# Another order of the query tiles in two causal attentions of a decoder trunk

## The chip, the core and the metric

The kernel runs on one core of one Trainium2 chip. The core has a matrix engine (TensorE, PE in the profile; PEld is its weight load), a vector engine (VectorE, DVE), a scalar engine (ScalarE, ACT), GpSimd (POOL) and a queue engine that issues most DMAs (SyncE, SP). Each engine runs its own instructions in their written order and waits on semaphores for the others. The metric is the device time of one launch in microseconds; lower is better.

## The reference, cut to what matters

Two decoder layers (DEPTH = 2) over 1024 positions of width 1024. Each layer is an RMSNorm, one input projection, four groups of heads side by side (Mamba-2 SSD, sparse attention "dsa", latent attention "mla", forgetting attention "fox"), an output projection with a residual, and a mixture of experts. The change touches mla and fox, which have four heads each and compute

```python
def one(i):                       # one tile of 128 queries
    start = i * Q_BLOCK           # Q_BLOCK = 128
    q_blk = lax.dynamic_slice_in_dim(q, start, Q_BLOCK, axis=1)
    logits = jnp.einsum('bqhd,bkhd->bhqk', q_blk, k) * scale
    ...                           # fox adds f_q - f_k
    mask = k_pos[None, :] <= q_pos[:, None]
    p = jax.nn.softmax(jnp.where(mask, logits, -jnp.inf), axis=-1)
    return jnp.einsum('bhqk,bkhd->bqhd', p, v)
```

The tiles are independent of each other. Tile t sees (t+1)·128 keys, so tile 7 is eight times as wide as tile 0.

## The kernel before, in words

A layer runs in phases with a barrier between them (PHASE, L293): projections and SSD, dsa, the latent up-projection (mla_proj, L935 to L948), then mla and fox as one run of `attend("mla", "fox")`, a barrier (phase "fox"), the output projection (L965) and the experts.

`attend` is written three times, once for each of PE (L729), ACT (L1121) and DVE (L1481). All three walk the same list `units` of (kind, tile t, head h), 64 entries for mla and fox: kind outermost, then tile, then head. Place u of the list does this:

- PE, `logits(u)`: the product of queries and keys for (t+1)·128 columns, in pieces of up to 512 (L753), and the diagonal mask (L758). It goes to one of two banks (`PS[n % 2]`), so it first waits until ACT has read the logits of place u-2 (L747, `lg_taken`).
- DVE: the row maximum over all (t+1)·128 columns (L1512) and its scaling (L1513).
- ACT: the exponential with its sum (L1151), which frees the bank (L1155).
- PE, `turn_p(u)`: t+1 transposes of 128x128 (L683), in turns of up to four. The turns go to ACT (L1086) and DVE (L1434) alternately, which copy them out of PSUM; a tile of five to eight blocks has two turns a head, and DVE has the second.
- PE, `pair_values(u)`, for two heads together: 4·(t+1) matmuls with the values (L782) and the spread of the reciprocal sums (L786). It waits for the copies of both heads.
- ACT `spread_sums` (L1137) and DVE `heads_out` (L1502), once per tile, the latter into the tile's own columns of `heads_cols`.

The three are staggered. In step s PE runs logits(s), then for even s pair_values(s-4), then turn_p(s-2) (L791 to L800). In step s DVE runs the maximum of s, then (at the fourth head) heads_out of the tile before, and only then the copies of s-2 (L1506 to L1523); its heads_out is left out for the first tile of the list (`NH < u`). ACT takes the copies of s-2, at the third head spread_sums, and then the exponential of s (L1139 to L1158). Buffers go by the place u in the list and not by the tile.

Of the kernel before, what the change touches and what calls it, by code (L numbers as in the profile page):

```python
# [27 lines left out]
T = SEQ // P  # L28
K = D // P
HALF = 512  # L30
NH, HD = 4, 64
# [44 lines left out]
def trunk(nc, x_in, positions, norm_mix, w_in, conv_w, conv_b, dt_bias, a_log, ssd_d, ssd_norm,  # L76
# [4 lines left out]
    with ctx:  # L81
# [39 lines left out]
        def g(off, *shape, dt=F32, parts=P):  # L121
            n = int(np.prod(shape))
            v = G[0:parts, off:off + n]
            if dt is not F32:
                v = v.bitcast(dt)
            if len(shape) == 2:
                v = v.rearrange("p (a b) -> p a b", a=shape[0])
            if len(shape) == 3:
                v = v.rearrange("p (a b c) -> p a b c", a=shape[0], b=shape[1])
            return v  # L130
# [3 lines left out]
        def bank(i):  # L134
            return PS[i // 2][:, (i % 2) * HALF:(i % 2 + 1) * HALF]
# [262 lines left out]
        }  # L398


        RL = g(0, T, 36)
        rw = g(288, K, 36)
        msk = g(576, T, EXPERTS)
# [270 lines left out]
        def _(pe):  # L674
# [24 lines left out]
            with pe.Fori(0, DEPTH) as l:  # L699
# [29 lines left out]
                def attend(*kinds, extra=None):  # L729

                    p, pT, _ = KINDS[kinds[0]]["at"]
                    units = [(kind, t, h) for kind in kinds for t in range(T) for h in range(NH)]

                    turned, first_o = {}, och.n
                    och.n += len(units)

                    def logits(u):
                        kind, t, h = units[u]
                        a = KINDS[kind]
                        if (kind, t, h) == ("fox", 0, 0):  # L740
                            pe.wait_ge(fox_rows_in, 16 * 2)
                            pe.wait_ge(fox_in, 48)
                        if kind == "dsa" and t >= 2 and h == 0:
                            pe.wait_ge(mask_ready, t - 1)
                        n = lg.next()
                        if n >= 2:
                            pe.wait_ge(lg_taken, n - 1)  # L747
                        L = PS[n % 2]
                        for c0 in range(0, (t + 1) * P, HALF):
                            c1 = min(c0 + HALF, (t + 1) * P)  # L750
                            by_choice = kind == "dsa" and t >= 2
                            diagonal = not by_choice and c1 == (t + 1) * P
                            m = pe.matmul(L[:, c0:c1], a["q"](h, t), a["k"](h, c0, c1), start=True,  # L753
                                          stop=not (by_choice or diagonal))
                            if by_choice:
                                m = pe.matmul(L[:, c0:c1], ident_h[:, :], chosen(t)[:, c0:c1], start=False, stop=True)
                            if diagonal:
                                m = pe.matmul(L[:, t * P:(t + 1) * P], ident_h[:, :], masks_h[:, 0, :], start=False, stop=True)  # L758
                        m.then_inc(lg_ready, 1)

                    def turn_p(u):

                        t = units[u][1]
                        pe.wait_ge(p_ready, first_o + u + 1)
                        turned[u] = []
                        for first in range(0, t + 1, 4):
                            n = min(4, t + 1 - first)
                            turned[u].append(turn([(i * P, P, p[:, u % 2, (first + i) * P:(first + i + 1) * P])
                                                   for i in range(n)]))

                    def pair_values(u):

                        kind, t, h = units[u]
                        tile, pair = (first_o + u) // NH, h // 2
                        O = bank(6 + tile % 2)
                        if pair == 0 and tile >= 2:
                            pe.wait_ge(o_taken, tile - 1)
                        for r in turned[u] + turned[u + 1]:
                            pe.wait_ge(tr_taken[r % 2], r // 2 + 1)
                        for b in range(t + 1):  # L780
                            for i in range(2):
                                pe.matmul(O[i * HD:(i + 1) * HD, pair * P:(pair + 1) * P], KINDS[kind]["v"](h + i, b),  # L782
                                          pT[:, (u + i) % 2, b * P:(b + 1) * P], start=(b == 0), stop=(b == t))
                        pe.wait_ge(sums_inverted, (first_o + u) // 2 + 1)
                        for i in range(2):
                            m = pe.matmul(O[i * HD:(i + 1) * HD, 256 + pair * P:256 + (pair + 1) * P],  # L786
                                          st_[:, (u + i) % 4, 3:4].to_broadcast([P, HD]), ident[:, :], start=True, stop=True)
                        if pair == 1:
                            m.then_inc(o_ready, 1)

                    for step in range(len(units) + 2):  # L791
                        if step < len(units):
                            logits(step)
                        if step >= 4 and step % 2 == 0:
                            pair_values(step - 4)
                        if 2 <= step:
                            turn_p(step - 2)
                        if step < len(units) and extra is not None:
                            extra(*units[step][1:])
                    pair_values(len(units) - 2)  # L800
# [262 lines left out]
        def _(act):  # L1063
# [45 lines left out]
            with act.Fori(0, DEPTH) as l:  # L1109
# [11 lines left out]
                def attend(*kinds, extra=None):  # L1121

                    p, pT, spread = KINDS[kinds[0]]["at"]
                    units = [(kind, t, h) for kind in kinds for t in range(T) for h in range(NH)]
                    last_turn, first_o = {}, och.n

                    def take_p(u):
                        t = units[u][1]
                        for first in range(0, t + 1, 4):
                            n = min(4, t + 1 - first)  # L1130
                            take(copy_to(pT[:, u % 2, first * P:(first + n) * P], width=n * P))
                        last_turn[u] = tr.n

                    def spread_sums(u):
                        tile = (first_o + u) // NH
                        act.wait_ge(o_ready, tile + 1)
                        act.activation(spread[:, tile % 2, :], bank(6 + tile % 2)[:, 256:512], ACT.Copy).then_inc(sums_spread, 1)  # L1137

                    for u in range(len(units) + 2):  # L1139
                        if u >= 2:  # L1140
                            take_p(u - 2)
                        if NH < u < len(units) and u % NH == 2:
                            spread_sums(u - 3)
                        if u < len(units):
                            kind, t, h = units[u]
                            n = lg.next()
                            o = och.next()
                            act.wait_ge(max_ready, o + 1)
                            if u >= 2:
                                act.wait_ge(tr_ready, last_turn[u - 2])  # L1150
                            act.activation(p[:, u % 2, 0:(t + 1) * P], PS[n % 2][:, 0:(t + 1) * P], ACT.Exp,  # L1151
                                           bias=st_[:, u % 4, 1:2], scale=KINDS[kind]["scale"],
                                           accum_out=st_[:, u % 4, 2:3]).then_inc(p_ready, 1)
                            act.wait_ge(p_ready, o + 1)
                            act.sem_inc(lg_taken, 1)  # L1155
                        if u < len(units) and extra is not None:
                            extra(*units[u][1:])
                    spread_sums(len(units) - 1)  # L1158
# [78 lines left out]
                i = 0  # L1237
# [153 lines left out]
        def _(dve):  # L1391
# [70 lines left out]
            with dve.Fori(0, DEPTH) as l:  # L1462
# [18 lines left out]
                def attend(*kinds, extra=None):  # L1481

                    p, pT, spread = KINDS[kinds[0]]["at"]
                    units = [(kind, t, h) for kind in kinds for t in range(T) for h in range(NH)]
                    first_o = och.n

                    def take_p(u):
# [18 lines left out]
                    for u in range(len(units) + 2):  # L1506
                        if u < len(units):
                            kind, t, h = units[u]
# [192 lines left out]
                i = 0  # L1701
# [132 lines left out]
                for t in (T - 2, T - 1):  # L1834
# [3 lines left out]
                dve.wait_ge(p2v, 2)  # L1838
                chain(dve.tensor_tensor(RL[:, :, :], bank(6)[:, 0:T * 36].rearrange("p (t e) -> p t e", t=T),
                                        rbias[:, :].unsqueeze(1).to_broadcast([P, T, 36]), ALU.add))  # L1840
# [166 lines left out]
```

## Time and profile before

| | |
|---|---|
| median of 3 runs | 3084.16 us (3083.2 to 3084.48) |
| the profiled execution's own time | 3082.44 us |
| its span, first to last instruction | 3080.7 us |
| mean granted TensorE clock | 0.906 |
| PE busy | 2610.5 us (85%) |
| DVE busy | 1381.8 us (45%) |
| ACT busy | 766.0 us (25%) |
| chain that ended last | PE 62%, DVE 22%, POOL 5%, issue 5%, ACT 4% |

The chain is the work that ended last, followed back from the last instruction; a share of it is time in which nothing else could have started the next piece sooner. The logits (L753) have 5%, the values (L782) 3% and the transposes of all stages (L683) 5% of it. The attention of the first layer stands in the trace from 762.15 us, when PE starts its first logits, to 928.03 us, when PE starts the output projection. The second layer's stands from 2280.9 to 2446.83 us.

### The profile page before, as it was taken

To read this page: it belongs to the slowest core of one execution; us is meant where nothing else is said; L and a number is where in the kernel's file an instruction comes from. 1 tells how busy PE (TensorE), PEld (TensorE's weight loads), DVE (VectorE), ACT (ScalarE), POOL (GpSimd) and SP (SyncE) were. 2 spreads that over 40 slices of the span, in tenths; PEclk is the share of its full clock that TensorE was granted. 3 is DMA by queue.
4 is the path that set the end of the run, shared out by engine and by line. 5 is a ranking of instruction groups with operands and counts; after the bars stand their busy time and mean duration, and the time that the engine had idled before them with its cause. 6 is when DMAs were issued, how large, how long until landed. Compare 5 with 4: busy or idle time off the path is not lost.

```text
span 3080.7 us, 30243 instructions
## 1 busy us (share of the span) xinstructions
PE 2610.5 (85%) x10356; PEld 1470.3 (48%) x10374; DVE 1381.8 (45%) x3164; ACT 766.0 (25%) x1630; POOL 375.7 (12%) x372
## 2 busy tenths in 40 slices
PE   5979768978999879999579897598889995999994
PEld 2564324545664534444335643245556644444442
DVE  4351498985551321111342516799755414111115
ACT  2121243144450111111112214321545311111112
POOL 0000177100000000000200003750000000000002
PEclk8989958999999889999789897599999997999996
DMA  5100001120000479999311000013010005799974
GB/s 212 39 28 23 28 1 40 41 84 32 11 1 16 165 263 336 333 332 336 144 57 52 1 23 28 0 50 113 2 42 1 10 28 212 285 336 336 335 260 177
DMA packets 105453, 370.42 MB, mean 120 GB/s; under 512 B 20754, under 2 KB 39912, under 8 KB 80744
## 3 DMA queue, kind: packets, MB, share of 16 engines
q1 hardware_dynamic: 91500, 318.41, 29.2%
q0 software_dynamic: 13824, 50.34, 4.3%
q8 instruction: 76, 1.25, 0.2%
q14 instruction: 53, 0.43, 0.0%
HBM read 304.42 MB, written 64.30 MB: 120 GB/s over the span
## 4 chain that ended last, share of the span: by engine, by line
PE 62%; DVE 22%; POOL 5%; issue 5%; ACT 4%; DMA 1%; DVEq 1%; ACTq 0%; SPq 0%; POOLq 0%
PE bank L1017 14%; PE bank L719 9%; PE bank L1034 8%; PE bank L965 7%; DVE group_arena L1671 7%; PE bank L722 6%; PE bank L753 5%; PE bank L683 5%; POOL group_arena L620 4%; PE bank L782 3%; DVE residual L1967 1%; PE bank L1024 1%; PE bank L978 1%; DVE softmax_stats L1512 1%; DVE group_arena L1445 1%
## 5 line engine op out<-in xcount | busy, mean ns | idle before, releaser
L719 PE MATMUL bank<-w_ring,normed_cols 128*128 128x260 f32 (+4 forms) x1280 | 419.0, 490 | 9.8 <-ACTq L1254 8.6
L719 PEld LDWEIGHTS bank<-w_ring,normed_cols 128*128 128x128 f32 x1280 | 245.9, 193 | 183.0 <-issue 158.3
L683 PE MATMUL bank<-ident,group_arena 128*128 128x128 f32 (+1 forms) x1200 | 198.0, 305 | 129.2 <-DVE group_arena L1445 59.8
L722 PE MATMUL bank<-normed_cols,w_ring 128*128 128x512 f32 x640 | 281.5, 601 | 15.5 <-DMA w_ring<-in_w_in 14.3
L640 POOL DMA_INDIRECT group_arena<-h_rows,group_arena x64 | 60.3, 942 | 1631.8 <-DVEq L1927 948.5
L1034 PE MATMUL bank<-heads_cols,group_arena 128*128 128x512 f32 x512 | 236.5, 604 | 7.8 <-DVE group_arena L1937 4.2
L914 PE MATMUL bank<-group_arena 64*128 64x512 f32 (+3 forms) x320 | 159.8, 814 | 95.7 <-ACTq L1254 93.8
L683 PEld LDWEIGHTS bank<-ident,group_arena 128*128 128x128 f32 (+1 forms) x1200 | 148.0, 154 | 189.1 <-issue 94.8
L1017 PE MATMUL bank<-w_ring,group_arena 128*128 128x512 f32 x512 | 230.5, 604 | 1.7 <-issue 1.7
L1017 PE MATMUL bank<-normed_cols,group_arena 128*128 128x512 f32 x512 | 224.9, 592 | 0.0
L965 PE MATMUL bank<-w_ring,heads_cols 128*128 128x512 f32 x512 | 222.6, 594 | 2.0 <-DVEq L250 2.0
L1935 DVE TENSOR_TENSOR group_arena<-group_arena,bank 128x256 f32<-128x256 f32 x64 | 27.0, 421 | 427.1 <-ACT group_arena L1351 427.1
L722 PEld LDWEIGHTS bank<-normed_cols,w_ring 128*128 128x128 f32 x640 | 122.8, 193 | 171.4 <-issue 156.3
L1671 DVE TENSOR_SCALAR_CACHE_REDUCE group_arena<-group_arena 128x768 bf16<-128x768 f32 (+4 forms) x260 | 196.9, 813 | 2.4
L1512 DVE TENSOR_REDUCE softmax_stats<-bank 128x1 f32<-128x128 f32 (+7 forms) x192 | 145.5, 758 | 116.8 <-PE bank L758 99.7
L753 PE MATMUL bank<-group_arena 96*128 96x512 f32 (+7 forms) x384 | 164.6, 528 | 32.5 <-ACTq L1155 28.2
L620 POOL TENSOR_SCALAR group_arena<-heads_cols,group_arena 128x1024 bf16<-128x1024 f32 x62 | 183.9, 2966 | 6.1
L1017 PEld LDWEIGHTS bank<-w_ring,group_arena 128*128 128x128 f32 x512 | 99.1, 194 | 127.3 <-issue 127.3
L914 PEld LDWEIGHTS bank<-group_arena 64*128 64x128 f32 x320 | 71.1, 276 | 182.6 <-ACTq L1254 143.8
L1017 PEld LDWEIGHTS bank<-normed_cols,group_arena 128*128 128x128 f32 x512 | 97.3, 190 | 122.5 <-issue 122.5
L965 PEld LDWEIGHTS bank<-w_ring,heads_cols 128*128 128x128 f32 x512 | 96.3, 190 | 119.1 <-issue 116.7
L1034 PEld LDWEIGHTS bank<-heads_cols,group_arena 128*128 128x128 f32 x512 | 92.0, 189 | 111.5 <-issue 96.9
(315 smaller groups left out, 3213.5 us busy)
## 6 DMA issues: line engine op xcount, KB each, us to landing
heads_cols<-in_expert_w_down SPq DMA_DIRECT2D x64, 1024.0 KB, 6.9
w_ring<-in_expert_w_gate SPq DMA_DIRECT2D x32, 1024.0 KB, 5.0
w_ring<-in_expert_w_up SPq DMA_DIRECT2D x32, 1024.0 KB, 7.7
normed_cols<-in_expert_w_gate SPq DMA_DIRECT2D x32, 1024.0 KB, 5.2
normed_cols<-in_expert_w_up SPq DMA_DIRECT2D x32, 1024.0 KB, 7.9
expert_rows<-group_arena SPq DMA_DIRECT2D x64, 512.0 KB, 7.2
w_ring<-in_w_in SPq DMA_DIRECT2D x6, 2048.0 KB, 8.4
expert_rows<-heads_cols SPq DMA_DIRECT2D x1, 8192.0 KB, 29.8
```

The lines of the kernel that those rows point to most:

```text
L620: pool.tensor_scalar(early_mask, flipped[T - 1], cand, None, ALU.is_ge).then_inc(early_masks, 1)
L683: last = pe.transpose(bank(4 + r % 2)[0:rows, col:col + src.shape[0]], src, ident[0:src.shape[0], 0:src.shape[0]])
L719: m = pe.matmul(proj_bank(n)[:, 0:width], HT[:, k, part * P:(part + 1) * P], w, start=(k == 0), stop=(k == K - 1))
L722: m = pe.matmul(proj_bank(n)[0:width, :], w, HT[:, k, part * HALF:(part + 1) * HALF], start=(k == 0), stop=(k == K - 1))
L753: m = pe.matmul(L[:, c0:c1], a["q"](h, t), a["k"](h, c0, c1), start=True, stop=not (by_choice or diagonal))
L782: pe.matmul(O[i * HD:(i + 1) * HD, pair * P:(pair + 1) * P], KINDS[kind]["v"](h + i, b), pT[:, (u + i) % 2, b * P:(b + 1) * P], start=(b = ...
L914: m = pe.matmul(PS[n % 2][:, c0:c1], qTi[lo:lo + 64, j // 2, t * P:(t + 1) * P], kTi[lo:lo + 64, c0:c1], start=True, stop=True)
L965: m = pe.matmul(bank(n % 4)[:, :], YT[:, k, t * P:(t + 1) * P], WR[:, slot, k, :], start=(k == 0), stop=(k == K - 1))
L1017: m = pe.matmul(bank(2 + s)[:, :], xgT[:, s, k, :], Wgu[w][:, :, k, :], start=(k == 0), stop=(k == K - 1))
L1034: m = pe.matmul(bank(6 + h)[:, :], aT[:, s, k, :], Wd[w][:, k, h * HALF:(h + 1) * HALF], start=(k == 0), stop=(k == 1))
L1512: chain(dve.tensor_reduce(st_[:, u % 4, 0:1], PS[n % 2][:, 0:(t + 1) * P], AX_X, ALU.max))
L1671: chain.go(dve.tensor_scalar(junk[t][:, 0:(t + 1) * P], src(t), limit(t), 0.0, ALU.is_ge, ALU.add, accum_out=thr[:, 0, t - 2:t - 1]))
```

## The change: what it does

A list of tiles in the order 7, 0, 6, 1, 5, 2, 4, 3 takes the place of 0 to 7 for mla and for fox, in the list `units` of all three engines. The first place of fox, which waits for the fox inputs, is now tile 7. The sparse attention keeps 0 to 7. No instruction is added, removed or resized.

```diff
+        LARGE_SMALL = [t for i in range(T // 2) for t in (T - 1 - i, i)]
+        TILE_ORDER = {"dsa": range(T), "mla": LARGE_SMALL, "fox": LARGE_SMALL}
...
                 def attend(*kinds, extra=None):
 
                     p, pT, _ = KINDS[kinds[0]]["at"]
-                    units = [(kind, t, h) for kind in kinds for t in range(T) for h in range(NH)]
+                    units = [(kind, t, h) for kind in kinds for t in TILE_ORDER[kind] for h in range(NH)]
...
-                        if (kind, t, h) == ("fox", 0, 0):
+                        if (kind, t, h) == ("fox", TILE_ORDER["fox"][0], 0):
                             pe.wait_ge(fox_rows_in, 16 * 2)
                             pe.wait_ge(fox_in, 48)
```

The line of `units` is changed in the same way for ACT (L1124) and for DVE (L1484).

## Rows read from the trace of the kernel before

**Rows 1.** Windows: span us, busy us (instructions) of PE, PEld, DVE, ACT, POOL; clock.
```profile
762.15:928.03 165.88, 155.43 (x1249) 106.13 (x1249) 86.61 (x224) 80.33 (x192) 0.00 (x0) 0.97 0.06 20
2280.90:2446.83 165.93, 155.45 (x1249) 106.12 (x1249) 86.61 (x224) 80.33 (x192) 0.00 (x0) 0.97 0.06 20
762.15:772.25 10.10, 9.35 (x41) 6.28 (x42) 4.06 (x18) 3.41 (x14) 0.00 (x0) 0.50 0.89 306
```
**Rows 2.** Waits of PE, 762 to 928.1: us in total, times, longest.
```profile
PE bank L782 <- DVE group_arena L1434: 4.5, 4, 1.6
PE bank L753 <- ACTq L1155: 4.0, 9, 0.6
```
**Rows 3.** Timeline, 836.9 to 848.5: start, us, instruction, [idle before <- releaser].
```profile
836.93 1.23 DVE L1512 TENSOR_REDUCE softmax_stats<-bank 128x1 f32<-128x1024 f32 x1 [1.09 <-PE bank L758]
...
838.26 0.41 DVE L1502 TENSOR_TENSOR heads_cols<-bank,group_arena 128x256 f32<-128x256 f32 x1
...
838.59 0.68 DVE L1434 COPY group_arena<-bank 128x512 f32<-128x512 f32 x1
...
839.42 1.97 PE L782 MATMUL bank<-group_arena 128*64 128x128 f32 x32 [1.37 <-DVE group_arena L1434]
...
844.95 1.97 PE L782 MATMUL bank<-group_arena 128*64 128x128 f32 x32 [0.59 <-DVE group_arena L1434]
...
848.42 0.70 PE L753 MATMUL bank<-normed_cols 66*128 66x256 f32 x2 [0.64 <-ACTq L1155]
```
**Rows 4.** DVE by line and form, 762 to 928.1: count, busy us, mean ns.
```profile
L1512 DVE TENSOR_REDUCE softmax_stats<-bank 128x1 f32<-128x1024 f32 x8 | 9.8, 1225 | 6.6 <-PE bank L758 6.6
L1512 DVE TENSOR_REDUCE softmax_stats<-bank 128x1 f32<-128x896 f32 x8 | 8.7, 1092 | 6.0 <-PE bank L758 6.0
L1434 DVE COPY group_arena<-bank 128x512 f32<-128x512 f32 x12 | 8.2, 686 | 10.4 <-PE bank L683 10.4
...
L1434 DVE COPY group_arena<-bank 128x384 f32<-128x384 f32 x12 | 6.6, 551 | 5.4 <-PE bank L683 5.4
```
**Rows 5.** Timeline, PE: logits of tiles 0 and 1; eight and four transposes.
```profile
842.97 1.10 PE L683 MATMUL bank<-ident,group_arena 128*128 128x128 f32 x8
...
843.91 0.39 PE L753 MATMUL bank<-normed_cols 66*128 66x128 f32 x2
...
849.86 0.60 PE L753 MATMUL bank<-normed_cols 66*128 66x256 f32 x2
...
868.37 0.60 PE L683 MATMUL bank<-ident,group_arena 128*128 128x128 f32 x4
```
**Rows 6.** Timeline, PE: logits that waited for ACT.
```profile
850.89 0.70 PE L753 MATMUL bank<-normed_cols 66*128 66x256 f32 x2 [0.26 <-ACTq L1155]
...
853.85 0.91 PE L753 MATMUL bank<-normed_cols 66*128 66x384 f32 x2 [0.53 <-ACTq L1155]
...
869.28 1.35 PE L753 MATMUL bank<-normed_cols 66*128 66x512 f32 x4 [0.31 <-ACTq L1155]
```
**Rows 7.** By line and form, ACT, 762 to 928.1, columns as in Rows 4.
```profile
L1151 ACT ACTIVATE group_arena<-bank,softmax_stats 128x896 f32<-128x896 f32 x8 | 8.1, 1007 | 1.1 <-DVE softmax_stats L1513 1.1
```
**Rows 8.** Timeline, PE: the end of the attention.
```profile
919.34 1.97 PE L782 MATMUL bank<-group_arena 128*64 128x128 f32 x32 [1.65 <-DVE group_arena L1434]
...
922.89 1.10 PE L683 MATMUL bank<-ident,group_arena 128*128 128x128 f32 x8 [0.34 <-ACT group_arena L1086]
...
924.87 1.97 PE L782 MATMUL bank<-group_arena 128*64 128x128 f32 x32 [0.88 <-DVE group_arena L1434]
...
928.03 2.41 PE L965 MATMUL bank<-w_ring,heads_cols 128*128 128x512 f32 x5 [0.98 <-DVEq L250]
```
**Rows 9.** Windows after a pause in the sparse attention, columns as in Rows 1.
```profile
717.60:721.00 3.40, 3.30 (x32) 3.33 (x34) 3.05 (x12) 0.27 (x2) 0.00 (x0) 0.51 0.00 0
721.00:724.40 3.40, 2.65 (x24) 1.91 (x20) 2.25 (x6) 1.19 (x2) 0.00 (x0) 1.00 0.00 0
```
**Rows 10.** Timeline, PE: values of the sparse attention's tile 7.
```profile
717.70 3.54 PE L782 MATMUL bank<-heads_cols,group_arena 128*64 128x128 f32 x32 [3.42 <-DVE heads_cols L1434]
```

More of the change, by code:

```diff
@@ L1123, in attend @@
                     p, pT, spread = KINDS[kinds[0]]["at"]
-                    units = [(kind, t, h) for kind in kinds for t in range(T) for h in range(NH)]
+                    units = [(kind, t, h) for kind in kinds for t in TILE_ORDER[kind] for h in range(NH)]
                     last_turn, first_o = {}, och.n
@@ L1483, in attend @@
                     p, pT, spread = KINDS[kinds[0]]["at"]
-                    units = [(kind, t, h) for kind in kinds for t in range(T) for h in range(NH)]
+                    units = [(kind, t, h) for kind in kinds for t in TILE_ORDER[kind] for h in range(NH)]
                     first_o = och.n
```

## The prediction, made before the changed kernel was run

> **What bounds the kernel now.** I read three views, in this order. First the windows of the two attention stretches, which are all that the change touches [rows 1]: 165.88 us in layer 0 and 165.93 us in layer 1, so one layer can stand for both. In it PE is busy for 155.43 us, DVE for 86.61 and ACT for 80.33. PE bounds the stretch, and the new order gives it the same matmuls. So it can only change three things: where PE waits, how much of its work runs at the low clock, and how the stretch ends. What is to be seen is that only 10.45 us of 165.88 are idle on PE. Perfect cover of all of it would bring 21 us in the two layers, or 0.7%.
>
> Second, the waits of PE [rows 2]. Values wait for DVE's copies four times, 4.5 us in total, and logits wait for ACT nine times, 4.0 us in total. The rest is at the end and in gaps under 0.2 us.
>
> Third, the timeline, which shows where they stand. The four waits of values are all behind a tile 7: two where mla's tile 7 is followed by fox's tile 0, 1.37 and 0.59 us [rows 3], and two at the very end, 1.65 and 0.88 us [rows 8]. Between tiles that grow by one there are none. The logits that wait are mostly the first of a tile behind tile 0, 1, 2 and 3: 0.64, 0.53, 0.42 and 0.31 us [rows 3, 6] (the 0.42 lies between the two rows shown; mla repeats the last three).
>
> **Why a fall in size costs.** PE runs logits(s), then values of s-4 and s-3, then transposes of s-2. With s the first head of the small tile, the values belong to the large one. They need DVE's copy of head s-3, and DVE makes that only behind the maximum of s-1, the last of the large tile. That maximum starts at 836.93, as soon as its logits are there, and takes 1.23 us; then come the scaling, heads_out at 838.26 and the copy of 0.68 us at 838.59; values start at 839.42 [rows 3]. PE can put into this time only eight transposes and the logits of tile 0, which is too little: 1.37 us idle. Two steps on, the values of the other two heads wait for DVE's copy of their last transposes, with only another short piece of logits between: 0.59 us [rows 3].
>
> **Part 1, falls in size.** Before there is one such fall, 7 to 0. The new order has four in each attention: 7 to 0, 6 to 1, 5 to 2, 4 to 3. I scale the first from the row. One tile less on the large side takes 0.13 us from the maximum and 0.13 us from DVE's second copy (1225 to 1092 ns, 686 to 551 ns) [rows 4], and takes one transpose from the cover, (1.10-0.60)/4 = 0.12 us; one tile more on the small side adds 0.21 us of logits to the cover (0.39 to 0.60) [rows 5]. The wait shrinks by 0.13+0.13-0.12+0.21, rounded 0.36 us a step: 1.37, 1.00, 0.63, 0.27. The second wait has no maximum and no transposes in it and shrinks by 0.13+0.21 = 0.34: 0.59, 0.25, 0, 0. One attention has 3.27+0.84 = 4.11 us. In mla the first fall lacks the heads_out, which the first tile of the list skips, and its 0.32 us (838.26 to about 838.59) [rows 3]: 3.79. Together 7.90, less the 1.96 of before: **+5.9 us a layer**. Bounds: if only the measured fall costs, twice, +1.6; if all eight falls cost as the first, +13.7. I take the scaled values, since the measured row lies on the same line and no instruction in it is new.
>
> **Part 2, the first logits behind a small tile.** ACT copies the first head, runs spread_sums and then the exponential of the third head, and the next tile's first logits need that bank. The chain is inside the small tile, so its neighbour doesn't shorten it. In fox the waits behind 0 to 3 become those behind 0 to 2, since 3 is last; in mla that behind tile 0 comes back at full clock. 0.64-0.31 [rows 3, 6]: **+0.3**.
>
> **Part 3, the third head of a tile.** Now it waits behind a small predecessor, as 0.26 us in tile 1 [rows 6]. Behind a large one this is gone, but 0 to 6 puts a new one in: maximum 1.09, exponential 1.01 [rows 4, 7] and some 0.5 for scaling, read and hand-overs, 2.6 us, against values and transposes of tile 0 (some 0.9) and one logits of tile 6 (0.39 + 6·0.21 = 1.6) [rows 5], 2.5 us. Behind 4, tile 3 is similar. A logits that waits also loses some 0.25 us of overlap with the transposes ahead of it. About as many go as come: **-0.2**, bounds -1.5 and +1.
>
> **Part 4, the end.** The stretch now ends on tile 3. Before, PE waited 1.65, 0.34, 0.88 and 0.98 us [rows 8]. With tile 3 the maximum is 0.53 us shorter and the cover of transposes 0.44 shorter, so 1.65 becomes 1.6; the 0.34 goes, since four blocks are one turn and nothing has to be freed; the other two stay. **-0.4**, bounds -1 and 0.
>
> **Part 5, the start and the clock.** Before, the first 10.10 us ran at a granted clock of 0.50, which is 1.2 GHz, with 9.35 us of PE busy, and got only through tile 0 and part of tile 1 [rows 1]. The same 32 matmuls of values take 3.54 us at the low clock and 1.97 at the full one [rows 10, 3], so at 2.4 GHz this work is 9.35·1.97/3.54 = 5.2 us; spread among large tiles, where short pieces overlap better, I take 4.9. So the old start costs 5.2 us over full speed. The new one starts with two logits of tile 7, 1.9 us each at full clock (0.39 + 7·0.21) [rows 5]. The nearest row of dense work behind a pause is the sparse attention's tail: values start at 717.70 behind 3.42 us of idle, the clock is low until 721.0 and then full [rows 9, 10]. By this row the clock rises some 3.3 us into the new start, with 1.6 us lost. The third logits need the first exponential: maximum 1.23, exponential 1.1 (its 1.01 at 896 columns, and one block more) [rows 3, 7], scaling, read and hand-overs some 0.6, together 2.9 us against 1.9 of cover; they wait 1.0 and lose the overlap, 0.4 more: 3.0 us. If it stays low twice as long, 3.3 us are lost and the wait is hidden. I take 3.1: **-2.1**, bounds -4 (no low clock) and 0 (low for 10 us as before).
>
> **Sum.** 5.9+0.3-0.2-0.4-2.1 = +3.5 us a layer, some +7 for two. On the execution's own 3082.44 us that is 3089.6; the median of the runs lies 1.7 us above this execution, so I predict 3091.3. The experts, the sparse attention and the projections get the same input at the same relative times; I put nothing there. SP's transfers at the start (w_out and the fox values) are waited for a whole attention later.
>
> **The rivals.**
> *Cover, faster.* A large tile's matmuls fill the idle time of the small one beside it. It decides from the point where the neighbour's work reaches into the small tile's four steps. For it: 165.88 less 155.43 leaves something to fill. Against it: PE reaches back only two to four heads and a tile has four in a row, and at 7 to 0 that very neighbour is the one that waits. If part 1 were nothing new (-1.96 instead of +5.9) and part 2 were gone as well (-3.4), a layer would be 8 us shorter: 3068 us. With half of it, 3075. Chance 0.05.
> *The clock pays for the falls.* At the new start the clock doesn't go down, or the falls 6 to 1 and below cost half. The start then costs 1.3 us, or part 1 is +4: +1.7 us a layer, 3087.6. For it: the low clock needs a pause ahead of it, the one before the sparse attention's tail was 3.42 us [rows 10], and no row says that the shorter ones around the barrier must bring it again. Chance 0.28, within 0.2%.
> *The clock goes down more often.* More pauses of 1 us on PE lower the granted clock inside the attention or at its end. Each 3.5 us at 1.2 GHz costs 1.6 us [rows 10, 3]; two a layer, +6.4, give 3098. Against it: 839 to 848.4 holds 2.6 us of such waits [rows 3], and the clock of the whole attention is 0.97, which the first 10.1 us at 0.50 make up alone (1-0.5·10.1/165.9) [rows 1]. Chance 0.12. The Trainium skill, "TensorE: Matmul & The Clock Gate", section "A second HAM failure mode: psum-queue depth-cycling", says that frequent short idles between groups of matmuls can make the clock swing; the trace here doesn't agree so far.
> *The forecast.* Slower by 4.5 to 10 us. Chance 0.55.
>
> **How the numbers follow.** About 0.2%, 6.2 us, is what a measurement of this kernel can tell from no change; the limit is at 3090.3. The forecast's own spread, from 3088.5 to 3094, puts some 0.07 of its 0.55 below the limit. Slower: 0.48+0.12 = 0.60; within: 0.28+0.07 = 0.35; faster 0.05. The range takes in the second rival and most of the third: 3085.5 to 3097.5.
>
> **What would show it.** Each fall shows as a wait of values for DVE's copy: 1.37, 1.0, 0.6, 0.3 and 0.6, 0.25. So values' waits for DVE rise from 4.5 to about 10.5 us in a layer. The attention of a layer lasts 169.4 us instead of 165.9. The low clock at its start lasts 3 to 7 us instead of 10.2. The last wait of values before the output projection stays at 0.9. The prediction is wrong if the stretch is shorter than 166 us, if the waits at 6 to 1 are absent (then DVE's order of work isn't the cause), if PE busy changes at full clock, or if the time changes outside the two stretches.

## The result, and the profile after

The changed kernel takes 3097.12 us (median of 6 runs, 3096.09 to 3099.57), the kernel before 3083.4 us (6 runs, 3077.54 to 3084.48). The ratio is 1.0048, 95% interval 1.0035 to 1.0061. The direction was forecast, the size wasn't: +13.7 us against +7. The span of the profiled execution is 3095.4 us, against 3080.7.

The windows of the two attention stretches of the changed kernel, and of the first 13.4 us of the first one (columns as in [rows 1]):

```profile
763.17:935.79 172.62, 158.12 (x1248) 106.66 (x1248) 85.92 (x224) 79.92 (x192) 0.00 (x0) 0.96 0.06 19
2288.98:2461.58 172.60, 158.10 (x1248) 106.68 (x1248) 85.88 (x224) 79.93 (x192) 0.00 (x0) 0.96 0.06 19
763.17:776.60 13.43, 13.43 (x24) 6.21 (x25) 4.68 (x7) 3.49 (x6) 0.00 (x0) 0.50 0.68 235
```

Against [rows 1] each layer is 6.7 us longer, 13.4 of the 14.7 us of the spans. It has two halves. PE is idle for 14.50 us instead of 10.45, which is +4.05. And it is busy for 158.12 us instead of 155.43 with the same matmuls, which is +2.69. I put that to the clock: the first 13.43 us run at 1.2 GHz, and PE is busy all through them, where before it was 10.10 us.

The waits of PE in the first stretch (to compare with [rows 2]):

```profile
PE bank L785 <- DVE group_arena L1437: 9.8, 12, 1.5
PE bank L756 <- ACTq L1158: 3.6, 7, 0.6
```

L785 is the values (L782 before), L1437 DVE's copies, L756 the logits. Values wait 9.8 us for DVE instead of 4.5. The timeline shows them at the falls in size; first mla's 7 to 0 with DVE beside it, then 6 to 1 and 5 to 2:

```profile
778.18 1.22 DVE L1515 TENSOR_REDUCE softmax_stats<-bank 128x1 f32<-128x1024 f32 x1 [1.44 <-PE bank L761]
779.51 0.68 DVE L1437 COPY group_arena<-bank 128x512 f32<-128x512 f32 x1
...
780.34 1.97 PE L785 MATMUL bank<-group_arena 128*64 128x128 f32 x32 [1.03 <-DVE group_arena L1437]
...
800.87 1.75 PE L785 MATMUL bank<-group_arena 128*64 128x128 f32 x28 [1.00 <-DVE group_arena L1437]
805.90 1.75 PE L785 MATMUL bank<-group_arena 128*64 128x128 f32 x28 [0.25 <-DVE group_arena L1437]
...
820.31 1.53 PE L785 MATMUL bank<-group_arena 128*64 128x128 f32 x24 [0.63 <-DVE group_arena L1437]
```

The end of the stretch, to compare with [rows 8], and its start:

```profile
930.28 1.09 PE L785 MATMUL bank<-group_arena 128*64 128x128 f32 x16 [1.55 <-DVE group_arena L1437]
933.50 1.09 PE L785 MATMUL bank<-group_arena 128*64 128x128 f32 x16 [0.88 <-DVE group_arena L1437]
935.79 1.55 PE L968 MATMUL bank<-w_ring,heads_cols 128*128 128x512 f32 x3 [0.98 <-DVEq L250]
```

```profile
760.93 1.42 PE L686 MATMUL bank<-ident,group_arena 128*96 128x128 f32 x8 [1.60 <-DVEq L1818]
763.17 3.78 PE L756 MATMUL bank<-group_arena 96*128 96x512 f32 x4 [0.82 <-DVEq L250]
766.75 0.31 PE L761 MATMUL bank<-masks_h,ident_h 128*128 128x128 bf16 x1
766.85 3.72 PE L756 MATMUL bank<-group_arena 96*128 96x512 f32 x4
770.37 0.31 PE L761 MATMUL bank<-masks_h,ident_h 128*128 128x128 bf16 x1
770.48 3.73 PE L756 MATMUL bank<-group_arena 96*128 96x512 f32 x4
774.00 0.31 PE L761 MATMUL bank<-masks_h,ident_h 128*128 128x128 bf16 x1
774.10 1.92 PE L686 MATMUL bank<-ident,group_arena 128*128 128x128 f32 x8
```

Three heads' logits of tile 7 follow each other without a gap, each in 3.6 us where full clock takes 1.8, and the clock doesn't come back. What is to be explained is that stretch. The forecast had it 3.3 us long.

### The profile page after: what moved, and what is told of

The parts are those of the page before. It is cut to its first block, busy times and chain, and to the rows that moved or that the text cites. A ratio compares the mean times of both kernels' runs of the same rounds, so it can differ in the third digit from the quotient of the medians.

```text
span 3095.4 us, 30243 instructions
## 1 busy us (share of the span) xinstructions
PE 2617.2 (85%) x10356; PEld 1472.5 (48%) x10374; DVE 1380.3 (45%) x3164; ACT 765.1 (25%) x1630; POOL 375.7 (12%) x372
## 4 chain that ended last, share of the span: by engine, by line
PE 62%; DVE 23%; POOL 5%; issue 5%; ACT 4%; DMA 1%; DVEq 1%; ACTq 0%; SPq 0%; POOLq 0%
PE bank L1020 14%; PE bank L722 9%; PE bank L1037 8%; PE bank L968 7%; DVE group_arena L1674 7%; PE bank L725 6%; PE bank L756 5%; PE bank L686 4%; POOL group_arena L623 4%; PE bank L785 3%; DVE residual L1970 1%; DVE softmax_stats L1515 1%; PE bank L1027 1%; PE bank L981 1%; DVE group_arena L1437 1%
## 5 line engine op out<-in xcount | busy, mean ns | idle before, releaser
L756 PE MATMUL bank<-group_arena 128*128 128x512 f32 (+7 forms) x384 | 171.5, 547 | 31.1 <-ACTq L1158 27.5
```

## The experiments

Each is named by what it does; ratios are to the kernel before, run on the same chip. The time of the attention of a layer, from PE's first logits of mla to the output projection, comes from the profile and tells more than the ratio, since the runs of a kernel scatter by several us.

**Narrow operands.** mla's queries and keys have 96 rows. Here the logits use all 128, the last 32 filled with zeros by GpSimd during the latent up-projection.

```diff
-q=lambda h, t: qTm[0:DQ, h, t * P:(t + 1) * P], k=lambda h, a, b: kTm[0:DQ, h, a:b]
+q=lambda h, t: qTm[:, h, t * P:(t + 1) * P], k=lambda h, a, b: kTm[:, h, a:b]
...
+                pool.wait_ge(roped, 4)
+                pool.memset(g(0, 2 * NH, SEQ)[DQ:P, :, :], 0.0).then_inc(rows_zero, 1)
```

> The changed kernel, with mla's logits taken over all 128 rows of the array (rows 96 to 127 of queries and keys hold zeros, so the result is the same) instead of 96. In the changed kernel the attention of a layer lasts 172.6 us and its first 13.4 us run at the low clock, PE being busy all the time. If the narrow operands keep the clock low (theory A), the clock rises about 3.3 us after the first logits and the attention lasts about 169 us, the kernel some 7 us less than the changed one. If the transfers beside it do (theory B), or if a low clock at this place lasts that long whatever runs (theory C), it stays at 172.6 us.

The ratio is 1.0046 (1.0029 to 1.0063), as the changed kernel's. But the attention of layer 0 lasts 167.30 us and has no low clock at all:

```profile
763.20:767.30 4.10, 1.31 (x9) 0.78 (x8) 2.95 (x9) 1.07 (x2) 0.00 (x0) 1.00 0.00 0
767.37:934.67 167.30, 151.69 (x1249) 103.95 (x1249) 85.82 (x224) 80.01 (x192) 0.00 (x0) 1.00 0.06 20
```

The first row is the pause ahead of it, with PE busy for 1.31 of 4.10 us. The second says what the attention is without the clock: 151.69 us of PE work, so the changed kernel loses 6.43 us a layer to it. The gain doesn't reach the kernel's time, because the up-projection beside the zeroing ends about 4 us later (first logits at 767.37 instead of 763.17). The trace shows where: while GpSimd zeroes, a copy on VectorE that takes 0.23 us elsewhere takes 5.21, and ends with the zeroing; PE waits 3.89 us for it.

```profile
737.93 6.92 POOL L639 MEMSET group_arena<- 32x8192 f32 x1 [118.46 <-DVEq L1822]
739.73 5.21 DVE L1821 COPY group_arena<-group_arena 128x128 f32<-128x128 f32 x1
```

The run is no test of theory A, since the clock never went down at this place and so couldn't come back. It shows something else: a pause of this kind is followed by a low clock in most runs, but not in every one.

**Transfers.** One line ahead of the load of the output projection's weights:

```diff
+                sp.wait_ge(o_taken, T + 2)
                 load_chunk(OUT_CHUNK)
```

> The changed kernel, with the loads of the output projection's weights and of fox's values issued two tiles later, when mla's second tile is done. Theory B (the low clock lasts as long as these transfers run, 762 to 773 us): the clock rises after 3 to 7 us, the attention lasts 169 to 170 us. Theories A and C: no change, 172.6 us with 13 us at the low clock.

```profile
764.25:777.70 13.45, 13.45 (x24) 6.23 (x25) 4.69 (x7) 3.50 (x6) 0.00 (x0) 0.50 0.00 1
764.25:936.90 172.65, 158.15 (x1249) 106.69 (x1249) 85.92 (x224) 79.93 (x192) 0.00 (x0) 0.96 0.06 19
```

In the low stretch the share of the DMA engines is 0.00 now, and it is 13.45 us long as before. Theory B falls. The ratio is 1.0049 (1.0032 to 1.0065).

**The pause.** Three matmuls whose result nobody reads, in PE's pause:

```diff
+                def busy(n):
+                    for _ in range(n):
+                        pe.matmul(bank(7), ident[:, :], ckvT[:, 0:HALF], start=True, stop=True)
+
+                busy(2)
                 turn_q_k(T - 1)
+                busy(1)
                 barrier(pe, PHASE["mla_proj"])
```

> The changed kernel, with three matmuls of 128x128 by 512 columns whose result nobody reads, put into PE's pause at the end of the latent up-projection: two ahead of the last turn of queries and keys, one behind it. If the pause there is what brings the low clock, it doesn't come, and the start costs only the wait of the third logits: the attention lasts about 167.5 us instead of 172.6, the kernel some 9 us less than the changed one. If the clock goes down all the same, it stays near 172.6, or is 1 us longer by the matmuls themselves.

```profile
755.00:762.00 7.00, 6.78 (x33) 3.95 (x32) 4.57 (x17) 3.34 (x8) 0.00 (x0) 1.00 0.00 0
763.02:930.30 167.28, 151.69 (x1248) 103.89 (x1248) 85.82 (x224) 80.01 (x192) 0.00 (x0) 1.00 0.06 20
```

PE is busy for 6.78 of the 7 us ahead of the barrier, the clock stays at 1.00, and the attention lasts 167.28 us, as expected (167.5); the third logits wait 1.09 us. The kernel is at 1.0014 (1.0004 to 1.0023) instead of 1.0048. So the low clock doesn't come when the pause is filled, in either layer, and 5.3 of the change's 6.7 us a layer hang on it. The pause alone isn't enough for it, as the run with 128-row logits shows.

**Fox alone.** `"mla": range(T), "fox": LARGE_SMALL`.

> The new order for fox alone; mla keeps 0 to 7. The attention then starts as before (10.2 us low) and has fox's four falls, except that mla's tile 7 is followed by fox's tile 7, so the fall between the two kinds is gone as well. Worked out from the changed kernel: falls 3.85 instead of 1.96, first logits behind a small tile less by about 0.3, third heads less by 0.4, end less by 0.4: +0.8 us a layer, 166.7 us, the kernel 1.5 us above the one before. If the low clock isn't tied to mla's order, about 170 us.

The attention lasts 166.25 us, 0.4 more than before, with 6.3 us of values waiting for DVE and 10.2 us at the low clock:

```profile
PE bank L785 <- DVE group_arena L1437: 6.3, 7, 1.5
```

The ratio is 1.0005 (0.9996 to 1.0015): no difference that can be measured.

**mla alone.** `"mla": LARGE_SMALL, "fox": range(T)`.

> The new order for mla alone; fox keeps 0 to 7. It has the start on tile 7 (13 us at the low clock, 1.9 us dearer than before by the changed kernel's trace), mla's falls (1.03+0.59+1.00+0.25+0.63 = 3.5 us), and tile 3 followed by fox's tile 0 in place of the fall of 7 to 0 (1.96). Sum: about 170 us, the kernel 8 us above the one before; with e4_fox_only it tells that the loss sits in mla's half. If the two halves are equally dear, about 168.5.

```profile
763.91:935.15 171.24, 158.45 (x1249) 106.56 (x1249) 86.32 (x224) 80.21 (x192) 0.00 (x0) 0.96 0.06 20
```

171.24 us, 5.4 more than before, and a ratio of 1.0035 (1.0023 to 1.0048). The loss sits in mla's half, where the start is. Of the 1.2 us over the expectation 1.0 is the step from mla's tile 3 to fox's tile 0, which I had priced at nothing: values wait 0.63 us there, and logits 0.36.

**What brings the clock back.** Eight unread matmuls (fp32, 512 columns) between the barrier and the first logits, over 128 rows and over 96:

```diff
                 barrier(pe, PHASE["mla_proj"])
+                for _ in range(8):
+                    pe.matmul(bank(7), ident[0:128, :], ckvT[0:128, 0:HALF], start=True, stop=True)
```

> The changed kernel, with eight matmuls of 128x128 by 512 columns (fp32, result not read) put between the barrier and the first logits of mla, behind the pause. They run at the low clock at first and use all 128 rows of the array. Theory A (operands of 96 rows don't bring the clock back): the clock rises some 3.4 us after the first of them and stays up, so the low stretch is at most 7 us long and the logits of tile 7 run at full speed. Theory C (a low clock here lasts 13.6 us whatever runs): the low stretch is 13.6 us, the logits are low still.

> The same with eight matmuls over rows 0 to 95 only, otherwise as long. Theory A: they do nothing for the clock; it stays low through them (6.9 us) and through tile 7's first three logits, 17 to 20 us in all, until transposes with 128 rows come. Theory C: 13.6 us as in the changed kernel. If dense work of any shape brings it back, at most 7 us as with 128 rows.

With 128 rows (first fence) the clock is back 3.2 us after the first of them, in both layers. With 96 rows (second fence) it takes 6.6 us in layer 0, and 4.0 us in layer 1 (the fence's last line), where it went down only 0.6 us behind the first matmul and not 0.2 us ahead of it:

```profile
761.26:764.50 3.24, 3.24 (x4) 1.51 (x5) 0.00 (x0) 0.00 (x0) 0.00 (x0) 0.51 0.51 157
764.50:769.80 5.30, 5.30 (x13) 2.29 (x12) 0.00 (x0) 0.00 (x0) 0.00 (x0) 1.00 1.05 388
```

```profile
763.18:766.40 3.22, 3.22 (x4) 1.51 (x5) 0.00 (x0) 0.00 (x0) 0.00 (x0) 0.50 0.55 174
766.40:769.80 3.40, 3.40 (x5) 1.35 (x4) 0.00 (x0) 0.00 (x0) 0.00 (x0) 0.50 1.05 403
769.80:773.40 3.60, 3.60 (x9) 1.52 (x8) 0.00 (x0) 0.00 (x0) 0.00 (x0) 1.00 1.03 337
...
2291.58:2295.60 4.02, 4.02 (x6) 1.72 (x7) 0.00 (x0) 0.00 (x0) 0.00 (x0) 0.58 0.66 222
```

So theory C falls: the length depends on what runs. The strong form of theory A falls too, since 96 rows alone do bring the clock back, only later. Single runs: 3103.05 and 3101.15 us, with 8.5 to 10.3 us of added matmuls a layer.

**The values that run through.** The same eight over 96 rows with mla's own queries and keys:

```diff
+                    pe.matmul(bank(7), qTm[0:DQ, 0, (T - 1) * P:], kTm[0:DQ, 0, 0:HALF], start=True, stop=True)
```

> As e5_dummy96, eight unread matmuls over 96 rows ahead of mla's first logits, but with the true queries and keys of tile 7 as operands in place of the identity and a row of latents; there is no diagonal mask between them. e5_dummy96 was back at the full clock 6.6 us (layer 0) and 4.0 us (layer 1) after its first matmul, the logits of the changed kernel only after 13.4 us. If what differs is the values that run through the array, the clock stays low through these eight as well and the low stretch is 13 us or longer. If it is the short mask between the logits, the clock comes back within 7 us as in e5_dummy96, and the first logits of tile 7 run at full clock: attention from its own first logits about 167 us.

```profile
763.36:770.00 6.64, 6.64 (x8) 2.85 (x9) 0.00 (x0) 0.00 (x0) 0.00 (x0) 0.50 0.80 281
770.00:773.60 3.60, 3.60 (x10) 1.52 (x9) 0.00 (x0) 0.00 (x0) 0.00 (x0) 1.00 1.07 352
```

6.64 us, the same in layer 1, and the attention from its own first logits lasts 167.19 us (a single run, 3105.26 us). The values made no difference. These eight and the changed kernel's logits, 6.6 against 13.4 us, still differ in more than one thing: the diagonal mask, a short bf16 matmul behind each head's logits; two PSUM banks in turn instead of one; and DVE and ACT, which read the logits meanwhile (4.68 and 3.49 us of the 13.43) and are idle beside the eight. I suspect the mask, but no run takes these apart, so it isn't shown which of them counts.

**Cause of the waits at the falls.** DVE's heads_out behind the copies of the same step:

```diff
-                        if NH < u < len(units) and u % NH == 3:
-                            heads_out(u - 4)
                         if u >= 2:
                             take_p(u - 2)
                             if u % 2 == 1:
                                 invert_sums(u - 3)
+                        if NH < u < len(units) and u % NH == 3:
+                            heads_out(u - 4)
```

> The changed kernel, with DVE's heads_out put behind the copies of the same step and not ahead of them. If each fall in size waits because DVE comes to the copy too late, the first wait of each fall that has a heads_out is 0.32 us shorter: 1.37, 1.00, 0.63 become 1.05, 0.68, 0.31, mla's first stays at 1.03, the one at the end goes from 1.55 to 1.23. Six such waits a layer: 172.6 becomes 170.7 us, the kernel 3.8 us less than the changed one. If the waits have another cause (the transposes, PSUM banks), nothing changes.

```profile
761.02:771.80 10.78, 10.78 (x17) 4.30 (x18) 2.86 (x5) 2.41 (x4) 0.00 (x0) 0.53 0.85 292
...
796.84 1.42 PE L785 MATMUL bank<-group_arena 128*64 128x128 f32 x22 [0.67 <-DVE group_arena L1437]
...
924.42 1.09 PE L785 MATMUL bank<-group_arena 128*64 128x128 f32 x16 [1.22 <-DVE group_arena L1437]
```

1.00 became 0.67 at 6 to 1, 1.55 became 1.22 at the end, 1.37 became 1.03, 0.63 became 0.30, and mla's 1.03 stayed at 1.04. PE's idle time fell from 14.50 to 12.5 us, about the 1.9 expected. So the first wait of each fall is set by when DVE comes to the copy; the second waits (0.59 and 0.25) stayed, as they should. The attention lasts 168.90 us, 1.8 less than I expected, since the clock was back 10.8 us after the first logits and not 13.4, although the same logits ran. It went down 0.5 us behind the first of them (0.7 in layer 1), in the changed kernel 0.2 us ahead. The sparse attention runs through the same code and changed with it, so the kernel's own time isn't a measure of this one place. The ratio is 1.0014 (1.0004 to 1.0024).

**Small falls only.** `"mla": range(T), "fox": range(T - 1, -1, -1)`.

> mla in the order 0 to 7, fox in the order 7 to 0, so no tile is followed by one that is more than one smaller. The fall of 7 to 0 (1.96 us) is gone and the stretch ends on tile 0 (about 1.4 us less waiting). By the formula of the falls, maximum + heads_out + copy + 0.3 less transposes less logits, falls by one tile cost nothing from 7 to 5 and then 0.15, 0.2, 0.7, 0.7, 0.8 us, some 2.6 in all. Sum: 1.0 to 1.5 us a layer less than before, 164.6 us, the kernel 2 to 3 us below the one before. If size differences cost in themselves and not by that formula, it is further below, 162 us.

```profile
762.65:925.36 162.71, 154.86 (x1249) 106.22 (x1249) 86.47 (x224) 80.30 (x192) 0.00 (x0) 0.97 0.06 21
```

162.71 us, 3.2 less than before and 1.9 less than I expected. The falls from 7 to 6, 6 to 5 and 5 to 4 cost 0.08, 0.14 and 0.20 us (expected 0, 0 and 0.15), that from 4 to 3 nothing (expected 0.2), and then come 0.27, 0.21 and 0.16 instead of 0.7 to 0.8: 1.1 us and not 2.6, so my formula is too dear from tile 4 down. The end waits 1.08, 0.47 and 0.98 us. The ratio is 0.999 (0.998 to 0.9999). Small steps down cost little; what costs is a large one.

**The old order without the pause.** The three matmuls of the pause in the kernel before.

> The kernel before (order 0 to 7 twice), with the three unread matmuls in PE's pause as in e3_prime. If the low clock at the start is brought by the pause and not by the order, it goes here too: the first 10.1 us, worth 5.2 us of work at full clock and some 1.5 to 2 us of waits of the small tiles, become about 7, and the attention lasts 163 us instead of 165.9, the kernel 5 to 6 us less. If the sparse work of tiles 0 and 1 lets the clock fall all the same, it stays at 165 to 166 us.

```profile
761.98:764.90 2.92, 2.01 (x14) 1.52 (x14) 1.24 (x6) 1.26 (x6) 0.00 (x0) 1.00 0.61 162
764.90:771.70 6.80, 6.39 (x30) 4.08 (x30) 2.73 (x12) 2.15 (x9) 0.00 (x0) 0.50 1.07 382
```

A miss. The clock is up for the first 3 us, in which tile 0 keeps PE busy for 2.01 of 2.92, and then goes down for 6.8 us (in layer 1 after 3.9 us, for 3.4). The attention lasts 165.3 us in layer 0 and 164.1 in layer 1; the ratio is 0.9997 (0.9987 to 1.0006), no difference. Here the clock falls with the small tiles at work, and filling the pause only puts that off and shortens it.

**All that helped.** mla 0 to 7, fox 7 to 0, heads_out behind the copies, and the pause filled.

> Three edits together: mla in the order 0 to 7 and fox 7 to 0, DVE's heads_out behind the copies, and the three unread matmuls in the pause. From e7_up_down's 162.7 us, 1.3 us less for the copies (waits of 0.14, 0.20, 0.27, 0.21, 0.16 and 0.32 of 1.08) and 3 us less for the clock, if both add up: 158.4 us, the kernel some 14 us below the one before. If the clock falls at the small tiles all the same, 161.4.

```profile
761.10:920.51 159.41, 152.05 (x1249) 104.36 (x1249) 86.14 (x224) 80.40 (x192) 0.00 (x0) 0.99 0.06 21
```

159.41 us, 6.5 less than before, 1.0 over the expectation; a low stretch of 3.4 us is left. The kernel takes 3065.13 us, ratio 0.9949 (0.9935 to 0.9963): it beats both the changed kernel and the one before. Of the 16.8 us between the spans (3063.9 and 3080.7) 13.2 lie in the two attentions.

## Why the prediction was right or wrong

**What bounds, and where it can change: right in the main.** The same matmuls on PE, and the time outside the two stretches moved by 1.3 us of 14.7. I had put nothing there; 1.0 of it stands ahead of the first attention, where both kernels run the same instructions.

**Part 1, falls in size: right.** Forecast in mla 1.05, 0.59, 1.00, 0.25, 0.63, 0.27 and in fox the same with 1.37; measured 1.03, 0.59, 1.00, 0.25, 0.63 and 1.37, 0.60, 1.00, 0.25, 0.63. Only the last, 4 to 3, isn't there. Together 7.35 us, +5.4 a layer against +5.9. The run with heads_out moved confirms the mechanism for the first waits. The run with small falls only shows where the scaling ends: from tile 4 down it is too dear.

**Part 2: right.** The first logits behind a small tile cost +0.4 (forecast +0.3).

**Part 3: -0.6 (forecast -0.2).** The old wait of 0.26 us went, the new one from 0 to 6 is 0.02 us. The rest of the -0.6 is gaps under 0.2 us, taken as what is left of PE's idle time when all named waits are counted.

**Part 4: right.** 1.55, 0.88 and 0.98 us at the end, -0.4 as forecast.

**Part 5, the start and the clock: wrong, and the error comes from here.** I gave the new start 3.1 us over full speed and the old one 5.2, -2.1 a layer. The new one loses 6.4 us, from 158.12 us of busy time to the 151.69 that two runs without the low clock show. Taken with the 0.74 us of waits that the old start had and the new one has not, the start is +1.95 (2.69-0.74) and not -2.1, 4 us a layer and 8 in all. The other parts came to +4.8 instead of +5.6, which by luck hid 1.6 of these 8. The step that failed is "By this row the clock rises some 3.3 us into the new start": it rose after 13.4. That is 3.3 of the 4 us. The other 0.7 is the old start, which set against the same 151.69 us cost some 4.5 (3.74 of busy time and 0.74 of waits, an estimate) and not 5.2.

The row [rows 9, 10] was matmuls over 128 rows with no mask between them; tile 7's logits have 96 rows and a mask behind each head. Where the clock fell 0.1 to 0.3 us ahead of the first matmul, it stayed low for 3.4 us with eight unread matmuls over 128 rows (two starts), 6.8 us over 96 rows (three starts) and 13.65 us with the logits (six starts: this kernel, the late transfers and mla alone). So the row was a measure of its own work and not of these logits. That the rows of the operands count is shown by the first two; what makes the logits longer still is open. I had bounded part 5 by "0 (low for 10 us as before)", and even this was too short. I put it at the end of the range for no better reason than that large tiles looked denser.

**The rivals.** *Cover, faster* is refuted by the falls: a large neighbour makes the small tile's steps wait. *The clock pays for the falls* had the start the wrong way round: the clock did go down there. Its price was about right where it doesn't, with the pause filled: +1.4 us a layer (167.28 against 165.88) for its +1.7, and the kernel within 0.2% (1.0014). *The clock goes down more often* named the right resource at the wrong place, and that its 3098 us lie near the measured 3097.12 is luck. No wait of 1 us at a fall brought the clock down in the changed kernel. But waits of this size can: behind the wait of 1.55 us at the very end of the attention the clock went down for 3.4 us in layer 1 of the run with 128-row logits and in both layers of the one with eight matmuls over 128 rows, and not in the other runs with the same wait. The Trainium skill, "TensorE: Matmul & The Clock Gate", section "A second HAM failure mode: psum-queue depth-cycling", describes a clock that swings under frequent short idles between groups of matmuls. In the changed kernel's two attentions the clock was low once each, at the start, so such a swing is not what cost the time here.

**Open.** The clock came back after 13.4 us in the changed kernel and after 10.8 with heads_out moved, with the same logits. What differs in the traces is where it fell: 0.2 us ahead of the first logits (low for 13.65 us) or 0.5 to 0.7 us behind them (low for 10.24 us), in both layers of each. The eight over 96 rows show the same: 6.83 us low when it fell 0.2 us ahead, 3.41 when it fell 0.6 us behind. So some half a microsecond in the place of the fall goes with 3.4 us in the length. Why is not shown, nor why the same kind of pause brought no low clock in the run with 128-row logits. There it can't be what ran behind the pause: the eight matmuls over 128 rows ran behind the pause too, and the clock had fallen before the first of them.

## What to carry to other kernels

When engines run one list in lockstep with a lag of a few steps, order the sizes so that no step goes down by much: the wide step's reduction and copy are still to be done when the narrow step offers no cover. Two short pauses ahead of a PE stage (1.6 and 0.8 us) cost 5.3 us here, because the stage then started at half clock; look at the granted clock in the first 15 us of a stage, and at what the engine streams there, before pricing a reordering of it. A row of dense work at the low clock was a fair measure only for work with the same rows, and even the same work differed by 2.6 us between starts, together with where the clock fell. Filling the pause pays only where dense work follows: ahead of the small tiles it gained 0.6 and 1.8 us in the two attentions and nothing that the kernel's time shows.

## What the runs showed of the hardware

How long the clock stays low under a PE that is always busy went with the work. From the first matmul to full clock it was 3.2 us with matmuls over 128 rows, 6.6 us (once 4.0) over 96 rows with either operands, and 10.8 to 13.6 us with 96-row logits and a short mask behind each head. In each of these the profile shows PE busy from the first matmul on, so busy time didn't tell how long the clock stayed low. Neither did the transfers beside it: 13.4 us at a DMA share of 0.68, 13.45 at 0.00. The shorter of two times for the same work (4.0 and 10.8) came where the clock fell 0.5 to 0.7 us behind the first matmul instead of 0.1 to 0.3 ahead.

A pause of 1.6 us, a turn of transposes and 0.8 us more ended in a low clock in every run that left it empty but one, that with 128-row logits, where the first pause was 1.89 us. With three matmuls in it the clock never fell there.

A copy of 128x128 on VectorE took 5.21 us instead of 0.23 while GpSimd cleared 32x8192 values (6.92 us), in both layers of the one run that has this memset beside it.
